# One FFN output turned onto the token axis: weights move, hidden stands, and the layers are written out

## The reference

```
D_MODEL, SEQ, DEPTH, D_FF = 2048, 256, 2, 5504
for l in range(DEPTH):
    h = rmsnorm(x, norm_mix[l])
    p = h @ w_in[l]
    x = x + concat(diff_attention(q, k, v), pool(a_in), conformer_conv(c_in)) @ w_out[l]

    h = rmsnorm(x, norm_ffn[l])
    gu = h @ w_ffn_in[l]
    g = causal_dwconv(gu[..., :D_FF], ffn_conv_w[l], ffn_conv_b[l])
    x = x + (silu(g) * gu[..., D_FF:]) @ w_ffn_out[l]
return rmsnorm(x, final_norm)      # x * rsqrt(mean(x*x) + 1e-6) * final_norm
```

## Time and profile before

| | |
|---|---|
| time, median of 3 runs | 2115.34 us (2114.9 to 2115.99) |
| the profiled execution's own time | 2115.62 us |
| its span | 2113.8 us |
| TensorE busy | 2081.6 us, 98% of the span |
| VectorE busy | 1438.0 us, 68% |
| ScalarE busy | 1086.7 us, 51% |
| GpSimd busy | 50.1 us, 2% |
| mean granted TensorE clock | 0.997 |
| DMA traffic | 391.76 MB, 185 GB/s over the span |

### The profile page before, as it was taken

How to read it: one execution, slowest core, us unless ns; L and a number is a source line. 1 busy time by engine, 2 the same in 40 slices (tenths; PEclk the granted TensorE clock), 3 DMA queues, 4 the chain that set the end, 5 groups by cost and what they waited for, 6 DMA issues and landing times.

```text
span 2113.8 us, 35281 instructions
## 1 busy us (share of the span) xinstructions
PE 2081.6 (98%) x11884; PEld 1808.3 (86%) x11884; DVE 1438.0 (68%) x2062; ACT 1086.7 (51%) x1516; POOL 50.1 (2%) x44
## 2 busy tenths in 40 slices
PE   9999999999999999999999899999999999999997
PEld 8877888888888888888888788888888888888886
DVE  7997767666666665555489977676666676655555
ACT  6447545555555554433463576455555555544334
POOL 0000100000000000000000001000000000001110
PEclk9999999999999999999999999999999999999999
DMA  8544465555555555555565444555555555555554
GB/s 285 170 160 150 143 196 179 198 186 194 189 179 188 197 185 193 192 197 184 195 212 180 158 140 161 191 190 188 190 187 179 198 189 189 189 190 196 194 196 140
DMA packets 108241, 391.76 MB, mean 185 GB/s; under 512 B 12144, under 2 KB 12656, under 8 KB 107888
## 3 DMA queue, kind: packets, MB, share of 16 engines
q1 hardware_dynamic: 105984, 384.87, 54.5%
q10 hardware_dynamic: 2160, 5.65, 0.8%
HBM read 388.38 MB, written 2.10 MB: 185 GB/s over the span
## 4 chain that ended last, share of the span: by engine, by line
PE 86%; DVE 7%; issue 5%; ACT 1%; DVEq 0%; DMA 0%; ACTq 0%
PE bank L1126 55%; PE bank L1129 27%; DVE gt L747 3%; PE bank L1213 2%; DVE wlo L686 2%; PE bank L1202 1%; PE bank L1204 1%; PE bank L1203 1%; DVE qT L692 0%; ACT whi L377 0%; DVE E L795 0%; DMA par<-params 0%; PE bank L1263 0%; DVEq L136 0%; ACT E L477 0%
## 5 line engine op out<-in xcount | busy, mean ns | idle before, releaser
L686 DVE TENSOR_TENSOR wlo<-raw,whi 128x1024 fp32r<-128x1024 f32 x728 | 891.9, 1231 | 618.8 <-ACT whi L377 615.1
L1126 PE MATMUL bank<-xg,whi 128*128 128x512 f32 x3648 | 1151.1, 397 | 9.4 <-DVE wlo L686 3.7
L377 ACT ACTIVATE whi<-raw 128x1024 fp32r<-128x1024 f32 x728 | 764.1, 1057 | 726.6 <-PE bank L1129 682.4
L1129 PEld LDWEIGHTS bank<-xg,wlo 128*128 128x128 f32 x3648 | 686.1, 188 | 162.2
L1129 PE MATMUL bank<-xg,wlo 128*128 128x256 f32 x3648 | 717.6, 278 | 0.0
L1126 PEld LDWEIGHTS bank<-xg,whi 128*128 128x128 f32 x3648 | 556.5, 189 | 13.8 <-DVE wlo L686 5.6
L1126 PE MATMUL bank<-hidden,whi 128*128 128x512 f32 x1376 | 427.1, 392 | 0.0
L1129 PEld LDWEIGHTS bank<-hidden,wlo 128*128 128x128 f32 x1376 | 258.4, 188 | 56.9
L1129 PE MATMUL bank<-hidden,wlo 128*128 128x256 f32 x1376 | 271.6, 279 | 0.0
L1126 PEld LDWEIGHTS bank<-hidden,whi 128*128 128x128 f32 x1376 | 208.4, 188 | 0.2 <-DVE wlo L686 0.2
L1126 PE MATMUL bank<-mix,whi 128*128 128x512 f32 x512 | 159.9, 394 | 0.5 <-DVE mix L873 0.5
(11 more groups left out here) (147 smaller groups left out, 897.0 us busy)
## 6 DMA issues: line engine op xcount, KB each, us to landing
raw<-wstream SPq DMA_DIRECT2D x729, 512.0 KB, 3.4
pw_sb<-pww ACTq DMA_DIRECT2D x2, 1024.0 KB, 6.6
x<-xT ACTq DMA_DIRECT2D x3, 512.0 KB, 10.6
outT<-x SPq DMA_DIRECT2D x3, 512.0 KB, 2.7
raw<-wstream SPq DMA_DIRECT2D x2, 256.0 KB, 3.9
x<-xT ACTq DMA_DIRECT2D x2, 256.0 KB, 5.4
poolw_sb<-poolw ACTq DMA_DIRECT2D x2, 256.0 KB, 6.6
outT<-x SPq DMA_DIRECT2D x2, 256.0 KB, 3.7
```

The costliest lines, as they stand in the source:

```text
L377: nc.scalar.activation(whi[:, s, :], raw[:, s, :], ACT.Copy).then_inc(hi_ready, 1)
L686: nc.vector.tensor_tensor(wlo[:, s, :], raw[:, s, :], whi[:, s, :], ALU.subtract).then_inc(lo_ready, 1)
L1126: nc.tensor.matmul(ps[bank][:], whi[:, s, blk * P:blk * P + P], mov, start=first, stop=False)
L1129: return nc.tensor.matmul(ps[bank][:, 0:S], wlo[:, s, blk * P:blk * P + P], mov[:, 0:S], start=False, stop=last)
```

## The change

It does four things.

- **Layers written out.** The loop over `l` is a Python loop on each engine: the code of a layer stands twice, with constants in its waits. The FFN loops inside stay, and so does the loop of the FFN output of layer 0.
- **The last FFN output by tokens.** In layer 1, `token_group` has 128 tokens of `hidden` as the stationary operand and streams `whi` and `wlo`, 512 columns wide, three products for a chunk and a token half, as in `v_group`. Group g writes banks 2g and 2g+1, with tokens on partitions.
- **The residual turned.** Behind eight pieces of that stage, `turn_x` transposes four blocks of `x` (4 chunks by 128 tokens) into bank 6 or 7, and ScalarE copies the bank to `xt` (`copy_turned`). `xt`, the gains as rows (one broadcast load, `load_gains`) and two small tiles lie where `xg` was.
- **The norm by scalars.** VectorE adds bank and `xt` (`token_sums`), ScalarE squares with an accumulator over the free axis (`token_squares`), VectorE multiplies three quarters by the gains (`token_gains`). After the last group: a sum of four numbers for a token, root, reciprocal, then one scale for a partition; 1536 columns of one token half on ScalarE, the other on VectorE (`FRONT`), the last 512 columns of both with their gains on VectorE. Four stores, tokens on partitions. GpSimd's and TensorE's parts of the final norm are gone.

The diff, cut to its core:

```diff
         x = sb("x", [P, KC, S])
-        xg = sb("xg", [P, KC, 2 * S], f32r)
+        with ExitStack() as until_ffn_out:
+            xg = sb("xg", [P, KC, 2 * S], f32r, until_ffn_out)
+        xt = sb("xt", [P, 2, DM])
+        gains = sb("gains", [P, DM])
...
+            for t in range(2):
+                sp.wait_ge(front_scaled[t], 1)
+                sp.dma_start(outT[:, t, 0:FRONT], xt[:, t, 0:FRONT]).then_inc(stored[t], 16)
+            for t in range(2):
+                sp.wait_ge(back_scaled, t + 1)
+                sp.dma_start(outT[:, t, FRONT:DM], xt[:, t, FRONT:DM]).then_inc(stored[2 + t], 16)
...
-            with act.Fori(0, LAYERS) as l:
+            for l in range(LAYERS):
...
+                def copy_turned(u):
+                    g, t = divmod(u, 2)
+                    act.wait_ge(x_turned, u + 1)
+                    nc.scalar.activation(xt[:, t, g * COLS:g * COLS + COLS], ps[6 + t][:], ACT.Copy).then_inc(x_copied, 1)
...
+                def token_squares(g):
+                    for t in range(2):
+                        act.wait_ge(evacuated, l * TILES + TD + 4 * g + (1 if t == 0 else NT) + CREDIT)
+                        nc.scalar.activation(y[:, 2 * t:2 * t + 2, :].rearrange("p a b -> p (a b)"),
+                                             xt[:, t, g * COLS:g * COLS + COLS], ACT.Square,
+                                             accum_out=ss[:, t, g:g + 1]).then_inc(token_squared, 1)
...
+                    for u in range(8):
+                        at(D0 + 11 + 4 * u, copy_turned, u)
+                    at(D0 + 14, load_gains)
+                    for g in range(3):
+                        at(D0 + DP * (g + 1) + 3, token_squares, g)
...
             nc.scalar.activation(credit[:, 0:1], eps[:, 0:1], ACT.Sqrt)
+            token_squares(3)
+            act.wait_ge(token_summed, 1)
+            nc.scalar.activation(rt[:], rt[:], ACT.Sqrt, bias=eps[:, 0:1], scale=1.0 / DM).then_inc(token_rms, 1)
+            act.wait_ge(token_rstd, 1)
+            nc.scalar.activation(xt[:, 0, 0:FRONT], xt[:, 0, 0:FRONT], ACT.Copy, scale=rt[:, 0:1]).then_inc(front_scaled[0], 1)
...
+                def token_sums(g):
+                    dve.wait_ge(x_copied, 2 * g + 2)
+                    for t in range(2):
+                        dve.wait_ge(acc_done, l * TILES + TD + 4 * g + t + 1 + DONE0)
+                        o = xt[:, t, g * COLS:g * COLS + COLS]
+                        nc.vector.tensor_tensor(o, ps[2 * g + t][:], o, ALU.add).then_inc(evacuated, 1 if t == 0 else NT - 1)
+
+                def token_gains(g):
+                    dve.wait_ge(gains_landed, 16)
+                    dve.wait_ge(token_squared, 2 * g + 2)
+                    o = xt[:, :, g * COLS:g * COLS + COLS]
+                    step(nc.vector.tensor_tensor(o, o, gains[:, None, g * COLS:g * COLS + COLS].to_broadcast([P, 2, COLS]),
+                                                 ALU.mult))
...
+            dve.wait_ge(token_squared, 8)
+            nc.vector.tensor_reduce(rt[:], ss[:], AX.X, ALU.add).then_inc(token_summed, 1)
+            dve.wait_ge(token_rms, 1)
+            nc.vector.reciprocal(rt[:], rt[:]).then_inc(token_rstd, 1)
...
+            nc.vector.tensor_scalar(xt[:, 1, 0:FRONT], xt[:, 1, 0:FRONT], rt[:, 1:2], None, ALU.mult).then_inc(front_scaled[1], 1)
+            for t in range(2):
+                nc.vector.scalar_tensor_tensor(out=xt[:, t, FRONT:DM], in0=xt[:, t, FRONT:DM], scalar=rt[:, t:t + 1],
+                                               in1=gains[:, FRONT:DM], op0=ALU.mult, op1=ALU.mult).then_inc(back_scaled, 1)
...
+                def turn_x(u):
+                    g, t = divmod(u, 2)
+                    if u < 2:
+                        pe.wait_ge(evacuated, l * TILES + TD + CREDIT)
+                    else:
+                        pe.wait_ge(x_copied, u - 1)
+                    for i in range(NT):
+                        last = nc.tensor.transpose(ps[6 + t][:, i * P:i * P + P], x[:, 4 * g + i, t * P:t * P + P], ident)
+                    last.then_inc(x_turned, 1)
+
+                def token_group(g):
+                    batches = [(p,) for p in range(DP - 2)] + [(DP - 2, DP - 1)]
+                    for batch in batches:
+                        order = [(p, kk, t) for p in batch for kk in range(2) if 2 * p + kk < FC for t in range(2)]
+                        if batch[0] == 0 or len(batch) == 2:
+                            order.sort(key=lambda o: o[2])
...
+                            xh = hidden[:, k, t * P:t * P + P]
+                            xl = hidden[:, k, S + t * P:S + t * P + P]
+                            wh = whi[:, s, kk * COLS:kk * COLS + COLS]
+                            wl = wlo[:, s, kk * COLS:kk * COLS + COLS]
+                            nc.tensor.matmul(bank, xh, wh, start=k == 0, stop=False)
+                            nc.tensor.matmul(bank, xh, wl, start=False, stop=False)
+                            last = nc.tensor.matmul(bank, xl, wh, start=False, stop=k == FC - 1)
...
+                if l == LAYERS - 1:
+                    for u in range(8):
+                        at(D0 + 8 + 4 * u, turn_x, u)
+                    for g in range(4):
+                        token_group(g)
+                    break
```

More of the change, by code:

```diff
@@ L313, in _ @@
                 load(LAYERS * PIECES // RING, s)
[L314 to L320, removed]
+            for t in range(2):
[4 more added lines that the diff above has]
+                sp.dma_start(outT[:, t, FRONT:DM], xt[:, t, FRONT:DM]).then_inc(stored[2 + t], 16)
+            for q in range(4):
                 sp.wait_ge(stored[q], 16)
@@ L677, in _ @@
             START = st.n
-            with dve.Fori(0, LAYERS) as l:
+            for l in range(LAYERS):
                 st.rebase(l * DVE_STEPS + START)
@@ L1021, in _ @@
                 pair_hooks(at, CJ, CT, TT, 6, CR)
-                for g in range(3):
-                    at(D0 + DP * (g + 1) + 2, residual_sums, g, TD + 4 * g, [4 * (g % 2) + i for i in range(NT)])
-                at(D0 + DP + 3, residual_lo, 0, 16, P_NN)
+                if l < LAYERS - 1:
+                    for g in range(3):
+                        at(D0 + DP * (g + 1) + 2, residual_sums, g, TD + 4 * g, [4 * (g % 2) + i for i in range(NT)])
+                    at(D0 + DP + 3, residual_lo, 0, 16, P_NN)
+                else:
+                    for g in range(3):
+                        at(D0 + DP * (g + 1) + 2, token_sums, g)
+                        at(D0 + DP * (g + 1) + 4, token_gains, g)
                 lo(2, 2)
@@ L1047, in _ @@
                 run(CT + 5, PIECES + 2)
[L1048 to L1060, removed]
+                if l < LAYERS - 1:
+                    residual_sums(3, TD + 12, [4 + i for i in range(NT)])
+                    SEEN["dve"] = st.n
+                else:
+                    token_sums(3)
+            dve.wait_ge(token_squared, 8)
+            nc.vector.tensor_reduce(rt[:], ss[:], AX.X, ALU.add).then_inc(token_summed, 1)
+            dve.wait_ge(token_rms, 1)
+            nc.vector.reciprocal(rt[:], rt[:]).then_inc(token_rstd, 1)
+            dve.wait_ge(token_rstd, 1)
+            settle()
+            nc.vector.tensor_scalar(xt[:, 1, 0:FRONT], xt[:, 1, 0:FRONT], rt[:, 1:2], None, ALU.mult).then_inc(front_scaled[1], 1)
+            for t in range(2):
+                nc.vector.scalar_tensor_tensor(out=xt[:, t, FRONT:DM], in0=xt[:, t, FRONT:DM], scalar=rt[:, t:t + 1],
+                                               in1=gains[:, FRONT:DM], op0=ALU.mult, op1=ALU.mult).then_inc(back_scaled, 1)
         @block.gpsimd
@@ L1066, in _ @@
             step, settle = st.step, st.settle
[L1069 to L1080, removed]
             pool.wait_ge(consts_loaded, 16)
             START = st.n
-            with pool.Fori(0, LAYERS) as l:
+            for l in range(LAYERS):
                 st.rebase(l * POOL_STEPS + START)
@@ L1122, in _ @@
                 nc.tensor.matmul(ps[7][:, 0:S], half[:, 0, 0:P], half[:, 0, :], start=True, stop=True)
-            with pe.Fori(0, LAYERS) as l:
+            for l in range(LAYERS):
                 def high_product(bank, s, blk, mov, first):
```

81 lines of the change are left out of this document (40 added, 41 removed).

## The result

The changed kernel takes 2126.22 us (median of 5 executions, 2124.54 to 2127.34) where the kernel before takes 2115.34. The ratio is 1.0047, interval 1.0035 to 1.0058: slower, by more than the 0.2% that can be told from no change. The forecast was 2109.4, range 2105.5 to 2113.0. The profiled execution took 2124.54 us.

The account below looks back on a forecast made before the run. TensorE, busy for 98% of the span, was taken as the bound. Products -3.4, turned residual +3.5, written-out layers -1.2 and the end -4.8 gave -5.9 us from 2115.34: 2109.4 us, range 2105.5 to 2113.0.

Parts of the forecast that it names:

- The products in the new form: Layer 1's FFN output: 1032 products at the value groups' 0.2270 us take 234.2 instead of 237.65 us, -3.4 us.
- rival 2: Last FFN output: the new form gains nothing with `hidden` as weights, term 0; 2112.8 us in all, chance 0.08.
- rival 4: Written-out layer 1 output stage: straight code starves TensorE, 22 gaps of 1.06 us, 23 us slower; 2133 us, chance 0.08.
- a spacing of 0.230 or more: Sign of a wrong forecast: product spacing in the last stage, where near 0.227 us was expected.
- The turned residual: Last FFN output: eight `turn_x` hooks of four transposes each delay TensorE by 0.44 us, +3.5 us.
- rival 3: `turn_x` hooks: transposes cost as much as full f32 products, +3.5 us more; 2112.9 us in all, chance 0.10.
- Copies, gains and token sums: Last FFN output: bank copies, the load of gains and the token sums stay hidden under TensorE's products, 0 us.
- Layers written out: Start of layer 1: TensorE's 1.23 us gap, taken as the jump back, goes, -1.2 us; bound 0.
- the 2.8 us of standing weight loads: TensorE's weight loads standing still in 10 places without releaser: 0 to -2.8 us possible from constant waits, taken as 0.
- rival 1: More from constants and the form: standing weight loads go, products run at their lower bound; -9.7, 2105.6 us, chance 0.08.
- The end: After the last product: first store issued at 3.88 us, stores take 7.1; 11.0 us instead of 15.8, -4.8 us.

Follow-up runs that it names:

- experiment 1: The changed kernel with its filler tile six floats shorter, so every tile lies at its old address: 2115.63 us, 0.9993 of the kernel before.
- experiment 5: A kernel of products only, other engines idle, with 17 distances between streamed and stationary tile, -256 to 256 bytes; wide products at negative distances averaged 232.1 ns.
- experiment 8: experiment 1 with 112 floats of padding ahead of `mix` and `hidden`, putting `hidden` at distance 0 from the weights: 2113.26 us, 0.9986 of the kernel before.
- experiment 2: The kernel before with eight floats (32 bytes) of padding between `xg` and the tiles behind it: 2125.26 us, 1.0045 of the kernel before.
- experiment 4: The kernel before with eight floats of padding ahead of `x`, so all tiles move together and distances stay: 2117.84 us, 1.0003 of the kernel before.
- experiment 10: experiment 1 without its eight `turn_x` transposes, `copy_turned` copying `x` as it stands (wrong residual): 2112.60 us, 0.9983 of the kernel before.
- experiment 9: The kernel before with only its four loops over layers written out: 2114.21 us, 0.9990 of the kernel before.

## Why the prediction was wrong

**The step that failed** is "The products in the new form": 0.2270 us from the value groups, with the reason that these "are the same instructions with another stationary tile". The other tile was the whole difference. In the value groups weights and `xg` lay at distance 0; in the new stage the streamed weights lie at -64 (192) from `hidden`, and the products took 0.2333: 240.8 us for 1032, where the pairs took 237.65. The term was +3.1 and not -3.4, 6.5 us off, even past the bound of 0 that rival 2 stood for. Experiments 1, 5 and 8 show it: the same form gives 0.2333, the distance alone does that, and with the distance changed 0.2270 appears. The prediction's support for the row was a chance: the two costs above the columns that it found so close, 12.7 ns for the old form on `hidden` and 13.6 for the value groups, belong to different distances, 64 and 0.

**A term that was missing** is the 32 bytes. The sum looked at the code that the diff touches, and held every other stage at its old time. The shift slows pairs on `xg` and value products in both layers: 10.6 us between the medians of the changed kernel and of experiment 1 (in the profiles 4.1 for each FFN input, 483.85 us against 479.73, and 0.95 for layer 1's input projection, 234.98 against 234.03: 10.1 for two layers). Experiments 1, 2 and 4 show it. No rival had it; rival 4 was slower too, but by gaps in the written-out code, and there are none. The prediction did name a spacing of 0.230 or more as a sign of being wrong, and that is what came.

The sum closes in the profiled executions. There the forecast was 2115.62 - 5.9 = 2109.7. With +6.5 for the form, +10.1 for the shift, +0.3 for the end, -0.8 for small savings in the stages that are now straight code (those of experiment 1 against the kernel before, outside the last stage), and -1.3 for the clock at the start, it is 2124.5; measured 2124.54.

**The turned residual**: right, 0.44 us each, +3.5; its transposes at full price (rival 3) are out, by the trace and by experiment 10. Copies, gains and token sums were hidden, as forecast.

**Layers written out**: right. The 1.23 us are gone (FFN output of layer 0: 237.38 us against 238.63). Of the 2.8 us of standing weight loads 2.1 are left, so rival 1 had at most 0.7 there; that is about the size of the small savings in the sum above.

**The end**: right, 11.3 for 11.0. The first store came 0.4 late: the hand-overs between the engines took 0.03 to 0.04, but the addition on VectorE starts 0.47 after the modelled end of the last product, where the forecast had 0.04. (The row that gave the 0.04 is between two VectorE instructions; that it also holds from engine to engine was luck.) The stores took 7.0 for 7.1. VectorE scaled 1536 columns in 1.02 us, not the 2.3 that stood as its bound; this changed nothing, as ScalarE's 1.57 sets the first issue.

The prediction weighed the Trainium skill ("TensorE: Matmul & The Clock Gate", section "Wait — 56ns, not 53.3ns?"), with its fixed cost of about 2.5 ns for a product. The runs show 13.4 to 21.0 ns above the 213.3 of 512 columns, by the distance. No run here shows 2.5, and the row of this case wasn't a constant either, though the sum treated it as one.

**What stays open**: why the distance counts. The runs show the pattern and its period of 256 bytes, for this data format and for products that each bring a new weight block; they don't show what in the memory or the weight load makes it. Nor do they show whether products that keep their weights are touched.

## What to carry to other kernels

Before a rate from one stage is carried to another, compare not only shapes and instructions but where both operands lie: here 32 bytes between them decided 3% of each wide product. When a change adds, drops or shrinks a tile, work out which later tiles move, and look at the spacing of starts in stages that the change doesn't touch: a stretch that is 100% busy in both kernels, with fewer instructions in the later one, is the sign. And it is a tuning knob: padding of 448 bytes alone brought 0.4%, more than the whole change was forecast to bring.

## What the runs showed of the hardware

- The spacing of 512-column products runs from 226.7 to 234.3 ns with the distance between the two operands modulo 256 bytes, that of four mixed ones from 691.4 to 703.3 (experiment 5). The two forms want different distances.
- Moving all tiles by 32 bytes changed no spacing, and other engines' work didn't make it: it is there with all of them idle (experiments 4 and 5).
- Four transposes of 128x128 float32 blocks, one behind the other, delay the next product by 0.36 us and the one behind it by 0.08 more (eight hooks of the changed kernel).
- At the start of an execution the granted clock from 9 to 13 us can be low (0.71 in the kernel before, 0.66 in experiment 1) or 1.00 (experiment 9, the changed kernel); it is worth 1.3 us. Where the clock column has no record yet it reads 1.00 all the same, and the count of starts tells (experiment 9).
- The jump back over a layer's code cost TensorE 1.23 us, and 1.5 to 2.5 in the profiles of five variants; in one of them the granted clock fell behind it (0.57 from 1055 to 1059 us). The FFN loops inside, which jump much less far, showed nothing: 428.00 of 428.00 us busy.
